# Turning a chunk's keys and scoring them in one TensorE product, with queries and identity side by side

## The chip, the core and the metric

One core of a Trainium2 chip runs the whole program. The metric is device time in microseconds (us) of one execution, the median of several runs. Engines are named as the profile names them: PE is TensorE's matmul, PEld its weight load, DVE is VectorE, ACT is ScalarE, POOL is GpSimd, SP is SyncE, which issues most DMAs.

## The reference

One streaming step of a layer: a SwiGLU half step, a mixer with eight heads (four mLSTM, four retention), an output projection, a second SwiGLU half step and a final norm, for 512 prompt frames and 32 sample frames with a model width of 1024. All in float32. The part that the change touches, for one chunk of one retention head:

```python
scores = einsum('bhtd,bhsd->bhts', q, k) * decay
inner = einsum('bhts,bhse->bhte', scores, v)
out = inner + cross[:, :, None] * einsum('bhtd,bhde->bhte', q, R)
tail = exp(lg[:, None] * (L - 1.0 - idx))
R_new = exp(lg * L)[:, None, None] * R + einsum('hs,bhsd,bhse->bhde', tail, k, v)
```

An mLSTM head has the same shape of work, with weights from its gates in place of `decay` and `tail`, and a normaliser beside the state.

## The kernel before

Activations lie with features on partitions and the T = 544 frames along the free axis; `P` is 128, `NC` is 4 (prompt chunks of 128 frames), `TS` is 32, `H` is 4. Weights arrive by DMA in `w_raw`, ACT rounds them to fp32r (`w_hi`) and DVE makes the remainder (`w_lo`); PE multiplies hi by hi, hi by lo and lo by hi (L763 for whole units of 1024 rows, L887 for the blocks of the feed-forward parts). Each engine's instructions stand in an order written out by hand, with semaphores between engines.

**The mixer** is a loop over eight heads. For each, PE makes four units: queries (u=0), keys (1), values (2), gate (3), each of 48 matmuls of 272 columns. DVE evicts a unit to `proj[:, h % 2, SLOT[what], :]`; in a retention head, queries and keys pass through `rot` and a GpSimd addition as well. The small work of a head is laid between the units of the next: `step_scores(h)` follows its own unit 3, `step_updates(h)` follows unit 0 of the next head, `step_mix(h)` unit 1, `step_turn(h)` the first product of unit 3. For the last head the output projection's units stand between.

**`step_scores` on PE** (L1064 on) fills the four PSUM banks of `X`: bank 0 the four chunks of keys, turned to frames on partitions (transposes against `ident`, L1087); bank 1 the values, turned (L1089); bank 2 the sample frames' keys and values (L1090, L1091) and the sample scores (L1094); bank 3 the chunks' scores, plain f32 products of keys and queries (L1093). The last of them raises `scores_done`.

**What reads them.** DVE's `step_scores` multiplies the scores by weights or decay into `scores` (L2277, L2286), makes the sample's entries (L2278, L2287, L2282, L2288, L2290) and, in mLSTM heads, the key tails `k_tail` (L2281), then raises `scores_weighted`. ACT's `step_values` copies the values to `v_tok` (L1597) and, in retention heads, makes the key tails first (L1595), then raises `v_ready`. The scores and tails are one buffer, `score_tail`, in the profile's names. PE's `step_updates` (L1103) waits for both and writes banks 0 and 1; DVE's `step_states` (L2305 on) follows.

**GpSimd** builds the mixer's constants once behind the first feed-forward part: `mask`, `sel` and a row of memsets, the last of which raises `mixer_consts`; ACT and DVE wait for that. `ident` lies beside `sq_sum` in `sum_ident` and is built at the program's start.

Of the kernel before, what the change touches and what calls it, by code (L numbers as in the profile page):

```python
# [7 lines left out]
ALU = mybir.AluOpType  # L8
ACT = mybir.ActivationFunctionType
# [3 lines left out]
P = 128  # L13
H = 4
# [30 lines left out]
def hybrid_trunk_step(nc, x_prompt, x_sample, state_mlstm_C, state_mlstm_n, state_mlstm_m, state_ret_R,  # L45
# [4 lines left out]
    TP, D = x_prompt.shape[1], x_prompt.shape[2]  # L50
    TS = x_sample.shape[1]
    T = TP + TS
# [4 lines left out]
    NC = TP // P  # L57
    CH = [slice(c * P, (c + 1) * P) for c in range(NC)] + [slice(TP, T)]
# [140 lines left out]
    with ExitStack() as ctx:  # L199

        at = {"next": -(-nc.sbuf_base // 32) * 32}

        def sb(name, shape, dt=F32):
            handle = nc.alloc_sbuf_tensor_at(name, shape, dt, offset=at["next"])
            at["next"] += -(-int(np.prod(shape[1:])) * 4 // 32) * 32
            return handle

        def sem(name):
            return ctx.enter_context(nc.semaphore(name))
# [9 lines left out]
        sq_sum, ident = sum_ident[:, 0:T], sum_ident[:, T:T + P]  # L219
# [82 lines left out]
        sel = sb("sel", [H, H, P])  # L302
        assert at["next"] <= y_ret_end
        at["next"] = y_ret_end
        proj = sb("proj", [P, 2, 4, T])
        table = sb("table", [P, tables.shape[1]])
        sel_r = sb("sel_r", [H, H, P], F32R)
        row_all = sb("row_all", [P, 2, T])
# [6 lines left out]
        weights = sb("weights", [P, T])  # L315
# [6 lines left out]
        scores = score_tail[:, 0:T]  # L322
        k_tail = score_tail[:, T:T + (NC + 1) * P].rearrange("p (c d) -> p c d", d=P)
        v_tok = sb("v_tok", [P, NC + 1, V1])
# [7 lines left out]
        assert at["next"] <= after_y_f  # L332
        at["next"] = after_y_f
        mask = sb("mask", [P, P])
        key_col = sb("key_col", [P, NC + 1, H])
        neg_m_exp = sb("neg_m_exp", [P, NC + 1, H])
        m_prev_all = sb("m_prev_all", [P, H, NC + 1])
        stats = sb("stats", [P, NC + 1, 6])
        mean_var = sb("mean_var", [P, NC + 1, 2])
        small = sb("small", [P, 7, NC + 1])  # L340
        mixer_end = at["next"]
        at["next"] = max(ffn_end, mixer_end)
        assert U_IN % RAW == 1 and 1 not in RAW_READ
# [7 lines left out]
        TAIL, TAIL_S = CROSS + H * P, CROSS + H * P + H  # L351
# [4 lines left out]
        X = ctx.enter_context(nc.psum_tensor("core_banks", [P, 4, 512], F32))  # L356
# [39 lines left out]
        SLOT = (3, 1, 2, 0)  # L396

        def projected(h, what):
            return proj[:, h % 2, SLOT[what], :]

        def sample_block(h, what):
            flat = proj[:, h % 2, :, :].rearrange("p a t -> p (a t)")
            a = SLOT[what] * T + TP
            return flat[:, a:a + P]
# [112 lines left out]
        table_loaded = sem("table_loaded")  # L517
        mixer_consts = sem("mixer_consts")
# [68 lines left out]
        def chained(eng, s):  # L587

            count = [0]

            def link(ins):
                count[0] += 1
                ins.then_inc(s, 1)
                eng.wait_ge(s, count[0])

            return link
# [153 lines left out]
        def _(pe):  # L750
# [317 lines left out]
            def p(h, what, cols):  # L1068
                return projected(h, what)[:, cols]

            def step_scores(h):


                if h >= H:
                    pe.wait_ge(rotated, 2 * (h - H) + 2)
                pe.wait_ge(evicted, T_IN + 4 * h + 3)
                if h:

                    pe.wait_ge(normed, h)
                    pe.wait_ge(normed_act, h)  # L1080
                else:
                    pe.wait_ge(past_ready, 1)
                if h:

                    pe.wait_ge(y_ready, h)
                for c in range(NC):
                    nc.tensor.transpose(X[:, 0, CH[c]], p(h, 1, CH[c]), ident[:, :])  # L1087
                for c in range(NC):
                    nc.tensor.transpose(X[:, 1, CH[c]], p(h, 2, CH[c]), ident[:, :])  # L1089
                nc.tensor.transpose(X[:, 2, 0:P], sample_block(h, 1), ident[:, :])  # L1090
                nc.tensor.transpose(X[:, 2, P:2 * P], sample_block(h, 2), ident[:, :])  # L1091
                for c in range(NC):
                    nc.tensor.matmul(X[:, 3, CH[c]], p(h, 1, CH[c]), p(h, 0, CH[c]), start=True, stop=True)  # L1093
                nc.tensor.matmul(X[:, 2, 2 * P:2 * P + TS], sample_block(h, 1), p(h, 0, CH[NC]),  # L1094
                                 start=True, stop=True).then_inc(scores_done, 1)

# [61 lines left out]
            for h in range(2 * H):  # L1158
                for u in range(4):
                    s, t = U_IN + 4 * h + u, T_IN + 4 * h + u  # L1160
# [56 lines left out]
        def _(act):  # L1217
            link = chained(act, act_step)
# [334 lines left out]
            c, half = X_BY_ACT  # L1553
            a = half * DT // 2
# [30 lines left out]
            def step_values(h):  # L1585
                act.wait_ge(scores_done, h + 1)
                if h:
                    act.wait_ge(mixed_done, h)
                if h == 0:
                    act.wait_ge(mixer_consts, 1)  # L1590
                if h == H:
                    act.wait_ge(table_loaded, 16)
                if h >= H:

                    nc.scalar.activation(k_tail[:, 0:NC, :], X[:, 0, :].rearrange("p (c d) -> p c d", c=NC), ACT.Copy,  # L1595
                                         scale=table[:, TAIL + h - H:TAIL + h - H + 1])
                nc.scalar.activation(v_tok[:, 0:NC, 0:P], X[:, 1, :].rearrange("p (c d) -> p c d", c=NC), ACT.Copy)\  # L1597
                    .then_inc(v_ready, 1)

            def step_gate(h):  # L1600
                act.wait_ge(evicted, T_IN + 4 * h + 4)
                if h:
                    act.wait_ge(y_ready, h)
                nc.scalar.activation(gate_act[:, :], projected(h, 3), ACT.Sigmoid if h < H else ACT.Silu)\
                    .then_inc(gate_act_ready, 1)
# [92 lines left out]
        def _(dve):  # L1698
            link = chained(dve, dve_step)
# [467 lines left out]
            for c, half in X_BY_DVE:  # L2167
                dve.wait_ge(x_moved, X_PIECES.index((c, half)) + 1)
                if c < NC:
                    tiles = dense[c % 2][:, half, :].rearrange("p (k d) -> p k d", d=P)  # L2170
                    a = half * DT // 2
# [98 lines left out]
            def step_scores(h):  # L2270
                dve.wait_ge(scores_done, h + 1)
                if h:
                    dve.wait_ge(mixed_done, h)
                grid = lambda ap: ap.rearrange("p (c d) -> p c d", c=NC)
                if h < H:
                    dve.wait_ge(weights_ready, h + 1)
                    nc.vector.tensor_tensor(scores[:, 0:TP], X[:, 3, :], weights[:, 0:TP], ALU.mult)  # L2277
                    nc.vector.tensor_tensor(scores[0:TS, TP:T], X[0:TS, 2, 2 * P:2 * P + TS], weights[0:TS, TP:T], ALU.mult)  # L2278

                    keep = grid(weights[:, 0:TP])[:, :, P - 1:P].broadcast_to([P, NC, P])  # L2280
                    nc.vector.tensor_tensor(k_tail[:, 0:NC, :], grid(X[:, 0, :]), keep, ALU.mult)  # L2281
                    nc.vector.tensor_scalar(k_tail[0:TS, NC, :], X[0:TS, 2, 0:P], weights[0:TS, T - 1:T], None, ALU.mult)  # L2282
                else:
                    d = DECAY + (h - H) * P
                    decay = table[:, d:d + P].rearrange("p (c d) -> p c d", c=1)
                    nc.vector.tensor_tensor(grid(scores[:, 0:TP]), grid(X[:, 3, :]), decay.broadcast_to([P, NC, P]), ALU.mult)  # L2286
                    nc.vector.tensor_tensor(scores[0:TS, TP:T], X[0:TS, 2, 2 * P:2 * P + TS], table[0:TS, d:d + TS], ALU.mult)  # L2287
                    nc.vector.tensor_scalar(k_tail[0:TS, NC, :], X[0:TS, 2, 0:P],  # L2288
                                            table[0:TS, TAIL_S + h - H:TAIL_S + h - H + 1], None, ALU.mult)
                nc.vector.tensor_copy(v_tok[0:TS, NC, 0:P], X[0:TS, 2, P:2 * P]).then_inc(scores_weighted, 1)  # L2290
# [89 lines left out]
            for h in range(2 * H):  # L2380
                for u in range(4):
                    s, t = U_IN + 4 * h + u, T_IN + 4 * h + u
# [49 lines left out]
        def _(pool):  # L2432
            link = chained(pool, pool_step)

            def triangle(ap, pattern, op, fill, base=0, mult=1):
                return nc.gpsimd.affine_select(out=ap, in_=ap, compare_op=op, fill=fill, base=base, pattern=pattern,
                                               channel_multiplier=mult)
# [56 lines left out]
            pool.wait_ge(w_lo_ready, U_IN + 1)  # L2494
            link(nc.gpsimd.memset(mask[:, :], 0.0))
            link(triangle(mask[:, :], [[1, P]], ALU.is_ge, -1e30, mult=-1))
            link(nc.gpsimd.memset(sel[:, :, :], 1.0))
            link(triangle(sel[:, :, :], [[-1, H], [0, P]], ALU.is_equal, 0.0))
            nc.gpsimd.memset(row_cols[:, :], 0.0)
# [105 lines left out]
```

## Time and profile before

| what | us |
| --- | --- |
| median of 3 runs | 1048.03 (1047.66 to 1048.28) |
| the profiled execution | 1047.74 |
| its span, first to last instruction | 1046.0 |
| PE busy in the span | 1033.6 |
| DVE, ACT, POOL busy | 791.3, 515.1, 215.8 |
| mixer's heads in the span | some 380 to 632 |

The span is what the trace covers; 1.74 us of the execution lie outside of it. Matmuls overlap, so a table's mean of one matmul is longer than its share of the time; the chain of waits lists pieces from start to start.

### The profile page before, as it was taken

Reading aid. Unit: us, or ns where it says so; the run is one execution under the profiler, and the core shown is the slowest. Engines: PE = TensorE matmul, PEld = TensorE weight load, DVE = VectorE, ACT = ScalarE, POOL = GpSimd, SP = SyncE. Lnnn points to the kernel's source line nnn. Section 1 sums busy time; section 2 is a strip of 40 time slices with the busy share of each in tenths; the row PEclk is TensorE's granted clock in tenths of the full one; section 3 lists DMA queues with packets and bytes.
Section 4 is the critical chain, followed back from the end, with each engine's and each line's share of the span. In section 5 each row is a group of like instructions: output and inputs, shape, how many; then the busy total and the mean of one; then the engine's idle time right before and its main releaser. Section 6 shows DMA issues by size and latency. Waiting matters only on the chain.

```text
span 1046.0 us, 20867 instructions
## 1 busy us (share of the span) xinstructions
PE 1033.6 (99%) x8229; PEld 1025.3 (98%) x8229; DVE 791.3 (76%) x1497; ACT 515.1 (49%) x943; POOL 215.8 (21%) x190
## 2 busy tenths in 40 slices
PE   9999999999999999999999999999999999999996
PEld 8999999999999999999999999999999999999996
DVE  5985689997899986555755556588568899789996
ACT  6453366644666664433232223445336664466654
POOL 1100221212122111310332223210012222221210
PEclk9999999999999999999999999999999999999998
DMA  7447787878878466445354223543777888887852
GB/s 226 115 80 181 173 178 167 181 171 174 179 163 172 100 136 137 79 65 84 65 81 76 68 79 62 142 91 86 177 162 165 172 175 170 178 178 167 175 107 97
DMA packets 217051, 142.13 MB, mean 136 GB/s; under 512 B 8685, under 2 KB 214677, under 8 KB 216825
## 3 DMA queue, kind: packets, MB, share of 16 engines
q1 hardware_dynamic: 160824, 110.98, 40.3%
q0 software_dynamic: 56048, 29.79, 22.3%
q8 instruction: 66, 1.08, 0.4%
q14 instruction: 33, 0.26, 0.1%
q10 hardware_dynamic: 80, 0.02, 0.0%
HBM read 135.80 MB, written 3.29 MB: 133 GB/s over the span
## 4 chain that ended last, share of the span: by engine, by line
PE 92%; DVE 3%; issue 2%; DMA 2%; ACT 1%; SPq 0%; DVEq 0%; ACTq 0%
PE dense L887 41%; PE dense L763 35%; PE core_banks L887 6%; PE core_banks L763 3%; PE dense L833 1%; PE core_banks L1118 1%; PE core_banks L1103 1%; DMA sum_ident<-sq 1%; PE core_banks L1121 1%; PE core_banks L1093 1%; DMA x_tok<-in_x_prompt 1%; DVE h_op L1811 1%; DVE w_lo L1769 1%; DVE h_raw L1799 0%; PE core_banks L1130 0%
## 5 line engine op out<-in xcount | busy, mean ns | idle before, releaser
L1306 ACT ACTIVATE w_hi<-w_src 128x512 fp32r<-128x512 f32 x182 | 113.2, 628 | 97.8 <-PE dense L887 55.7
L1306 ACT ACTIVATE w_hi<-w_raw 128x512 fp32r<-128x512 f32 x182 | 112.4, 629 | 77.6 <-PE dense L887 52.1
L887 PE MATMUL dense<-h_op,w_hi 128*128 128x272 f32 x768 | 147.8, 291 | 0.8 <-DVE h_op L1811 0.8
L1769 DVE TENSOR_TENSOR w_lo<-w_src,w_hi 128x512 fp32r<-128x512 f32 x182 | 124.6, 689 | 29.9 <-ACT w_hi L1306 28.1
L1769 DVE TENSOR_TENSOR w_lo<-w_raw,w_hi 128x512 fp32r<-128x512 f32 x182 | 123.9, 688 | 29.0 <-ACT w_hi L1306 27.0
L763 PE MATMUL dense<-xg_hi,w_hi 128*128 128x272 f32 x672 | 141.6, 292 | 0.0
L763 PE MATMUL dense<-xg_hi,w_lo 128*128 128x272 f32 x672 | 138.4, 288 | 0.0
L763 PE MATMUL dense<-xg_lo,w_hi 128*128 128x272 f32 x672 | 138.1, 287 | 0.0
L887 PE MATMUL dense<-x_late_hi,w_hi 128*128 128x272 f32 x432 | 125.7, 291 | 0.0
L887 PE MATMUL dense<-x_op_hi,w_lo 128*128 128x272 f32 x432 | 124.6, 288 | 0.0
L887 PE MATMUL dense<-x_late_hi,w_lo 128*128 128x272 f32 x432 | 124.5, 288 | 0.0
L887 PE MATMUL dense<-x_op_hi,w_hi 128*128 128x272 f32 x432 | 124.4, 288 | 0.0
L887 PE MATMUL dense<-x_late_lo,w_hi 128*128 128x272 f32 x432 | 124.1, 287 | 0.0
L887 PE MATMUL dense<-x_op_lo,w_hi 128*128 128x272 f32 x432 | 124.1, 287 | 0.0
L887 PEld LDWEIGHTS dense<-h_op,w_hi 128*128 128x128 f32 x768 | 120.1, 188 | 3.3 <-DVE xT L1898 2.8
L1713 DVE TENSOR_TENSOR w_lo<-w_raw,w_hi 128x1024 fp32r<-128x1024 f32 (+1 forms) x69 | 86.3, 1251 | 38.1 <-ACT w_hi L1252 37.9
L887 PE MATMUL dense<-h_op,w_lo 128*128 128x272 f32 x384 | 110.7, 288 | 0.0
L763 PEld LDWEIGHTS dense<-xg_lo,w_hi 128*128 128x128 f32 x672 | 105.1, 188 | 0.0
L763 PEld LDWEIGHTS dense<-xg_hi,w_lo 128*128 128x128 f32 x672 | 104.8, 189 | 0.0
L763 PEld LDWEIGHTS dense<-xg_hi,w_hi 128*128 128x128 f32 x672 | 104.6, 189 | 0.1
L1252 ACT ACTIVATE w_hi<-w_raw 128x1024 fp32r<-128x1024 f32 (+1 forms) x69 | 68.9, 1000 | 30.8 <-PE dense L763 17.2
L887 PEld LDWEIGHTS dense<-x_late_hi,w_hi 128*128 128x128 f32 x432 | 81.2, 188 | 2.1 <-DVE rstd L1844 2.1
(363 smaller groups left out, 2389.4 us busy)
## 6 DMA issues: line engine op xcount, KB each, us to landing
w_raw<-in_w_ffn_up SPq DMA_DIRECT2D x43, 512.0 KB, 5.0
w_src<-in_w_ffn_gate SPq DMA_DIRECT2D x36, 512.0 KB, 5.2
w_raw<-in_w_in SPq DMA_DIRECT2D x31, 512.0 KB, 8.4
w_src<-in_w_ffn_gate POOLq DMA_DIRECT2D x36, 256.0 KB, 5.5
w_raw<-in_w_ffn_up POOLq DMA_DIRECT2D x36, 256.0 KB, 6.0
w_src<-in_w_ffn_down SPq DMA_DIRECT2D x16, 512.0 KB, 5.3
w_raw<-in_w_ffn_down SPq DMA_DIRECT2D x16, 512.0 KB, 5.2
w_raw<-in_w_ffn_down SPq DMA_DIRECT2D x16, 384.0 KB, 5.8
```

What stands on the lines that cost most here:

```text
L763: last = nc.tensor.matmul(out[:, half, 0:TH], w[:, s % 4, k, :], x(kt)[:, half * TH:(half + 1) * TH], start=start and n == 0 and m == 0, s ...
L833: last = nc.tensor.matmul(bank_of(u)[:, half, 0:TH], w[:, u, k, :], x(k)[:, half * TH:(half + 1) * TH], start=part == "hh" and k == 0, sto ...
L887: last = nc.tensor.matmul(out, w[:, k, :], x, start=o in OPENS and k == 0 and m == 0, stop=k == KH - 1 and m == 2, skip_group_check=o not ...
L1093: nc.tensor.matmul(X[:, 3, CH[c]], p(h, 1, CH[c]), p(h, 0, CH[c]), start=True, stop=True)
L1103: last = nc.tensor.matmul(X[:, b, o * V1:(o + 1) * V1], k_tail[:, c, :], v_tok[:, c, :], start=True, stop=True)
L1118: last = nc.tensor.matmul(out, score_tail[:, block], v_tok[:, c, :], start=True, stop=c == 0)
L1121: last = nc.tensor.matmul(out, sum_ident[:, block], state, start=False, stop=True)
L1252: nc.scalar.activation(w_hi[:, s % 4, 0:k_tiles(s), :], raw, ACT.Copy).then_inc(w_hi_ready, 1)
L1306: nc.scalar.activation(block_of(w_hi, n, o), source(e, o), ACT.Copy).then_inc(block_hi, 1)
L1713: nc.vector.tensor_tensor(w_lo[:, s % 4, 0:nk, :], unit_raw(s), w_hi[:, s % 4, 0:nk, :].bitcast(F32), ALU.subtract).then_inc(w_lo_ready, 1)
L1769: nc.vector.tensor_tensor(block_of(w_lo, n, o), source(g % 2, o), block_of(w_hi, n, o).bitcast(F32), ALU.subtract)\
L1811: nc.vector.tensor_tensor(lo, h_source(k, o), hi.bitcast(F32), ALU.subtract).then_inc(h_op_lo_ready, 1)
```

## The change

The identity gets a second copy, `ident_near`, right behind `proj` in one buffer, `proj_wide`, built by GpSimd. A chunk's key product then has keys as the stationary operand and a moving operand of two pieces of 128 columns, queries and identity, so that one plain product of 256 columns writes the chunk's scores and its turned keys side by side. `KEY_CHUNKS` spans banks 0 and 1 of `X`; the values move to bank 3. PE's four key transposes and four score products per head become four such products. PE waits for `mixer_consts` before the first head's. In retention heads the key tails move from ACT to DVE. The small per-chunk tables are packed into one buffer (`minis`), which makes room for the second identity.

```diff
-        proj = sb("proj", [P, 2, 4, T])
+        proj_region = at["next"]
+        proj_wide = sb("proj_wide", [P, 2 * (2 * 4 * T + P) - 3 * T])
+        proj = proj_wide[:, 0:2 * 4 * T].rearrange("p (n a t) -> p n a t", n=2, a=4)
+        ident_near = proj_wide[:, 2 * 4 * T:2 * 4 * T + P]
+        at["next"] = proj_region + (2 * 4 * T + P) * 4
...
+        minis = sb("minis", [P, (NC + 1) * (3 * H + 15)])
...
+        def query_and_ident(h, c):
+
+            q = (h % 2) * 4 * T + SLOT[0] * T + c * P
+            stride = 2 * 4 * T - q
+            return proj_wide[:, q:q + 2 * stride].rearrange("p (a s) -> p a s", a=2)[:, :, 0:P]
+
+        KEY_CHUNKS = X[:, 0:2, :].rearrange("p a b -> p (a b)").rearrange("p (c a d) -> p c a d", c=NC, a=2)
+        SCORES_OF, KEYS_OF = KEY_CHUNKS[:, :, 0, :], KEY_CHUNKS[:, :, 1, :]
...
+                if h == 0:
+                    pe.wait_ge(mixer_consts, 1)
                 for c in range(NC):
-                    nc.tensor.transpose(X[:, 0, CH[c]], p(h, 1, CH[c]), ident[:, :])
+                    nc.tensor.matmul(KEY_CHUNKS[:, c, :, :], p(h, 1, CH[c]), query_and_ident(h, c), start=True, stop=True)
                 for c in range(NC):
-                    nc.tensor.transpose(X[:, 1, CH[c]], p(h, 2, CH[c]), ident[:, :])
+                    nc.tensor.transpose(X[:, 3, CH[c]], p(h, 2, CH[c]), ident[:, :])
                 nc.tensor.transpose(X[:, 2, 0:P], sample_block(h, 1), ident[:, :])
                 nc.tensor.transpose(X[:, 2, P:2 * P], sample_block(h, 2), ident[:, :])
-                for c in range(NC):
-                    nc.tensor.matmul(X[:, 3, CH[c]], p(h, 1, CH[c]), p(h, 0, CH[c]), start=True, stop=True)
...
-                if h == H:
-                    act.wait_ge(table_loaded, 16)
-                if h >= H:
-
-                    nc.scalar.activation(k_tail[:, 0:NC, :], X[:, 0, :].rearrange("p (c d) -> p c d", c=NC), ACT.Copy,
-                                         scale=table[:, TAIL + h - H:TAIL + h - H + 1])
-                nc.scalar.activation(v_tok[:, 0:NC, 0:P], X[:, 1, :].rearrange("p (c d) -> p c d", c=NC), ACT.Copy)\
+                nc.scalar.activation(v_tok[:, 0:NC, 0:P], X[:, 3, :].rearrange("p (c d) -> p c d", c=NC), ACT.Copy)\
...
-                    nc.vector.tensor_tensor(scores[:, 0:TP], X[:, 3, :], weights[:, 0:TP], ALU.mult)
+                    nc.vector.tensor_tensor(grid(scores[:, 0:TP]), SCORES_OF, grid(weights[:, 0:TP]), ALU.mult)
...
-                    nc.vector.tensor_tensor(k_tail[:, 0:NC, :], grid(X[:, 0, :]), keep, ALU.mult)
+                    nc.vector.tensor_tensor(k_tail[:, 0:NC, :], KEYS_OF, keep, ALU.mult)
...
-                    nc.vector.tensor_tensor(grid(scores[:, 0:TP]), grid(X[:, 3, :]), decay.broadcast_to([P, NC, P]), ALU.mult)
+                    nc.vector.tensor_tensor(grid(scores[:, 0:TP]), SCORES_OF, decay.broadcast_to([P, NC, P]), ALU.mult)
...
+                    nc.vector.tensor_scalar(k_tail[:, 0:NC, :], KEYS_OF, table[:, TAIL + h - H:TAIL + h - H + 1], None, ALU.mult)
...
+            link(nc.gpsimd.memset(ident_near[:, :], 0.0))
+            link(triangle(ident_near[:, :], [[-1, P]], ALU.not_equal, 1.0))
```

## Rows read from the trace of the kernel before

**Rows 1.** The page: busy time by engine; shares of the chain that ended last.

```profile
PE 1033.6 (99%) x8229; PEld 1025.3 (98%) x8229; DVE 791.3 (76%) x1497; ACT 515.1 (49%) x943; POOL 215.8 (21%) x190
...
PE 92%; DVE 3%; issue 2%; DMA 2%; ACT 1%; SPq 0%; DVEq 0%; ACTq 0%
```

**Rows 2.** PE's waits over the whole span: us in total, times, longest.

```profile
PE dense L1057 <- DMA x_tok<-in_x_prompt: 1.3, 1, 1.3
PE dense L1024 <- ACT x_gain L1496: 1.2, 1, 1.2
PE core_banks L1024 <- DVE xT L1898: 1.2, 1, 1.2
...
PE dense L763 <- issue: 0.3, 1, 0.3
```

**Rows 3.** Busy time by stretch (us, instructions in brackets), granted clock, DMA share, GB/s.

```profile
core 0: us, PE busy (x) PEld busy (x) DVE busy (x) ACT busy (x) POOL busy (x), PEclk, DMA share, GB/s
...
526.00:556.00 30.00, 30.00 (x248) 30.00 (x248) 17.59 (x39) 8.36 (x11) 10.14 (x7) 1.00 0.50 82
...
sum 240.00, PE 240.00 PEld 239.72 DVE 137.94 ACT 75.35 POOL 56.93; mean PE 26.67 PEld 26.64 DVE 15.33 ACT 8.37 POOL 6.33
```

**Rows 4.** Chain of waits, a retention head's scores and updates: start, us, what.

```profile
526.25 0.44 PE core_banks L1087 x4
...
527.34 0.89 PE core_banks L1093 x8
528.23 0.14 PE core_banks L1094 x2
...
534.45 1.11 PE core_banks L1103 x10
```

**Rows 5.** PE by line and shape: xcount | busy us, mean ns of one | idle before.

```profile
L1093 PE MATMUL core_banks<-proj 128*128 128x128 f32 x64 | 8.5, 275 | 0.0
...
L1087 PE MATMUL core_banks<-sum_ident,proj 128*128 128x128 f32 x32 | 4.8, 272 | 0.0
```

**Rows 6.** Chain of waits at the second feed-forward block's norm sums.

```profile
674.20 0.92 PE core_banks L808 x4
```

**Rows 7.** Instructions in time, same head: DVE, then ACT; start, us, what [idle before].

```profile
528.41 0.69 DVE L2286 TENSOR_TENSOR score_tail<-core_banks,table 128x512 f32<-128x512 f32 x1 [1.27 <-PE core_banks L1094]
...
529.38 0.27 DVE L2290 COPY v_tok<-core_banks 32x128 f32<-32x128 f32 x1
530.57 1.23 DVE L1713 TENSOR_TENSOR w_lo<-w_raw,w_hi 128x1024 fp32r<-128x1024 f32 x1 [0.92 <-ACT w_hi L1252]
...
528.41 0.69 ACT L1595 ACTIVATE score_tail<-core_banks,table 128x512 f32<-128x512 f32 x1 [3.48 <-PE core_banks L1094]
529.00 0.59 ACT L1597 ACTIVATE v_tok<-core_banks 128x512 f32<-128x512 f32 x1
```

**Rows 8.** Instructions in time, DVE, in an mLSTM head.

```profile
498.62 0.71 DVE L2210 TENSOR_TENSOR proj<-dense,rstd 128x544 f32<-128x544 f32 x1
...
499.95 0.67 DVE L2281 TENSOR_TENSOR score_tail<-core_banks,weights 128x512 f32<-128x512 f32 x1
```

**Rows 9.** Last head: chain of waits at the updates; DVE in time.

```profile
620.96 1.11 PE core_banks L1103 x10
...
618.87 0.27 DVE L2290 COPY v_tok<-core_banks 32x128 f32<-32x128 f32 x1
```

**Rows 10.** Instructions in time, mixer's start: GpSimd, then ACT's first user.

```profile
379.89 0.20 POOL L2495 MEMSET mask<- 128x128 f32 x1 [11.33 <-DVE w_lo L1713]
...
381.12 0.52 POOL L2497 MEMSET sel<- 4x512 f32 x1
...
383.57 0.10 POOL L2509 MEMSET state_in<- 128x4 f32 x1
...
393.16 0.61 ACT L1659 ACTIVATE sel_r<-sel 4x512 fp32r<-4x512 f32 x1
```

More of the change, by code:

```diff
@@ L334, in hybrid_trunk_step @@
         mask = sb("mask", [P, P])
[L335 to L340, printed above, removed]
+        tables_of = {}
+        minis = sb("minis", [P, (NC + 1) * (3 * H + 15)])
+        first = 0
+        for name, inner in (("key_col", H), ("neg_m_exp", H), ("stats", 6), ("mean_var", 2)):
+            tables_of[name] = minis[:, first:first + (NC + 1) * inner].rearrange("p (c a) -> p c a", a=inner)
+            first += (NC + 1) * inner
+        for name, outer in (("m_prev_all", H), ("small", 7)):
+            tables_of[name] = minis[:, first:first + (NC + 1) * outer].rearrange("p (a c) -> p a c", a=outer)
+            first += (NC + 1) * outer
+        key_col, neg_m_exp, m_prev_all = (tables_of[name] for name in ("key_col", "neg_m_exp", "m_prev_all"))
+        stats, mean_var, small = (tables_of[name] for name in ("stats", "mean_var", "small"))
         mixer_end = at["next"]
```

## The prediction, made before the changed kernel ran

> **What bounds the kernel now.** Read the page's busy shares and its chain of work first [rows 1]: TensorE (PE) is busy for 1033.6 of 1046.0 us and carries 92% of the chain that ended last. A busy PE is not by itself a bound, so read PE's waits over the whole span next [rows 2]: there are six lines of them, 5.9 us in all (the first three and the last are shown), and the three longest are PE's first work (L1057, input frames) and its last (L1024, the turned output). None belongs to a line of the mixer's heads. The table by stretches confirms it [rows 3]: over the nine stretches from 400 to 640 us PE is busy for 240.00 of 240 us, and in the one shown, as in the others, the granted clock is 1.00 (the higher level, 2.4 GHz), while VectorE (DVE) is busy for about 58% and ScalarE (ACT) for about 31% (137.94 and 75.35 of 240.00). So in the mixer, time is PE's time: an operation that PE gains moves the end by its spacing to the next, and an operation that DVE or ACT gains or loses costs nothing until PE waits for it.
>
> The durations of single matmuls (0.27 us) overlap, so they are of no use as prices. The chain of waits gives start-to-start pieces, and its pieces for one head [rows 4] are the prices: four key turns (L1087) 0.44 us, the four score products (L1093) 0.89. The score products have eight instructions: the table by line [rows 5] has 64 for 32 products (L1093), but 32 for 32 turns (L1087). A plain f32 product is thus two passes over its columns, each with its own weight load, and a turn is one. That gives 0.44/4 = 0.110 us for a turn and 0.89/8 = 0.111 us for a pass of 128 columns.
>
> **The change on PE.** Per head it removes the four key turns and the four score products, 0.44 + 0.89 = 1.33 us; the value turns stay, into another bank. It adds four plain f32 products of 256 columns, eight passes. What is a pass of 256 f32 columns worth? The trace has one wide f32 product: the norm's sums at L808, two halves of 272 columns, four passes in 0.92 us [rows 6], 0.230 each. Between 0.111 at 128 columns and 0.230 at 272 the line has a slope of 0.119/144 = 0.00083 us a column, so 256 columns take 0.111 + 128 x 0.00083 = 0.217 us; 0.230 x 256/272 gives the same. Eight of them: 1.736 us. The head therefore pays 1.736 - 1.33 = +0.41 us. The saved weight loads bring nothing, since they ran under the columns: the pass of 32 columns at L1094 takes 0.14/2 = 0.07 us [rows 4], so a load with its product fits into 0.07, and 0.111 at 128 columns is the columns' own time. In short, keys are no longer turned in the one-pass mode but in the two-pass mode of a product, and that doubles the turn: 4 x (0.217 - 0.110) = 0.43, less a few nanoseconds of spacing per instruction. Eight heads: 8 x 0.406 = **+3.2 us**.
>
> No row shows a moving operand in two pieces as far apart as queries and identity. At the dear end it runs as two pieces of 128: 0.222 a pass, 64 x 0.222 - 8 x 1.33 = +3.6 us. A gain would need a pass under 1.33/8 = 0.166, and 272 columns took 0.230, so that end is left to rival 1. I take +3.2, by L808, the nearest row in width and type.
>
> Beside the row stands a rule: the Trainium skill ("TensorE: Matmul & The Clock Gate", Terms) calls the transpose mode four times faster for FP32. It speaks against this change as the rows do, but its factor is not theirs: rows 4 make it 0.222/0.110 = 2 for 128 columns; with its factor the same edit would cost 32 x (0.440 - 0.110) = +10.6 us (an estimate from that page).
>
> **DVE and ACT.** In the four retention heads ACT loses the key tail (L1595, 0.69 us) and DVE gains it. The nearest DVE rows are the same step's products from PSUM with as many elements: 0.69 (L2286) [rows 7] and 0.67 (L2281) [rows 8]. I take +0.7; the low end is the 0.27 of L2290, which has a quarter of the columns. Cover: before, DVE's last step (L2290) ends at 529.38 + 0.27 = 529.65 and ACT's copy of the values at 529.00 + 0.59 = 529.59, and PE wants both only at 534.45, when the updates (L1103) start [rows 4, 7]. With +0.7 DVE ends at 530.35, 4.1 us early. The next instruction in DVE's queue, a w_lo (L1713), starts at 530.57 after 0.92 us of waiting for ACT's w_hi, which stands behind the work that ACT loses; so it isn't later either. The tightest case is the last head, where only half a unit of products stands between: updates at 620.96, DVE's end at 618.87 + 0.27 = 619.14 [rows 9]. With +0.7 for DVE, and PE's extra 0.41 shifting both sides alike, 1.1 us remain. Price: 0. If the cover were gone, 4 x 0.7 = 2.8 us. In the four mLSTM heads DVE's operations stay; they read other places in PSUM, in rows of 128 with gaps, as the eviction L2210 already reads two pieces in two banks: 0.71 us for 544 [rows 8], no dearer per element than L2281. Price: 0.
>
> **GpSimd and the new wait.** Two more instructions build the second identity behind the mask. Mask's pair takes from 379.89 to 381.12, when sel's starts: 1.23 us [rows 10]. The last memset, which raises mixer_consts, goes from 383.57 to 384.80. The first user of mixer_consts is ACT's sel_r at 393.16: 8 us of cover. DVE waits for it ahead of the gate rows; behind the memset in GpSimd's queue stands a DMA of these very rows, and PE, whose wait is new, stands before the first head's scores, behind products that need them (L1138, L1146). So the condition is met when PE comes to it, though all of PE's later work stands behind that wait. Price: 0, or 1.2 us once without cover. No DMA is added or moved; the 512 bytes by which later buffers shift, and the small tables packed into one, change no instruction.
>
> **Sum.** Profiled execution: 1047.74 us with a span of 1046.0, so 1.74 lie around it. New span 1046.0 + 3.2 = 1049.2, execution 1050.9. The median of the runs is 0.29 above that execution: **1051.2 us**.
>
> **Rivals.**
> 1. Weight loads set the pass. If 0.111 us were the load and not the columns, a pass of 256 would cost no more than one of 128: eight passes 0.89, and the change would save the four turns, 8 x 0.44 = 3.5 us: 1044.5, faster. It decides wherever a load is longer than the columns' time. For it: the load rows are as busy as the product rows [rows 3]. Against it: 0.07 at 32 columns, 0.111 at 128 and 0.230 at 272 grow with columns. Chance 0.04. The Trainium skill's same page (Back-to-back issue gap) has sustained pairs grow from about 81 to 131 ns between 128 and 512 columns, which leans to this side; rows 4 and 6 do not agree with it for f32, where twice the columns take twice the time.
> 2. The added time is taken up elsewhere. If PE's 0.41 a head replaced a wait further on, the end would move by 1 us or less: 1048 to 1049, no measurable change. For it: some waits exist. Against it: none is in the mixer, and the few behind it hang on PE's own results, which come later by the same amount [rows 2]. Chance 0.05.
> 3. DVE becomes late. If the key tails had no cover, the updates of four heads would wait 0.7 each: 1051.2 + 2.8 = 1054.0. Against it: 1.1 to 4.1 us of slack. Chance 0.03.
> 4. Turning by plain product costs four times a turn rather than twice (the rule above as a mechanism: 0.440 for a 128-column product). 1058.6. Against it: score products of the same type cost 0.222. Chance 0.01.
>
> **How the numbers follow.** Forecast, +2.6 to +4.0 us: 0.87. A change of 0.2% (2.1 us) is about what a measurement of this kernel can tell from none. Slower: forecast 0.87 + rival 3 0.03 + rival 4 0.01 = 0.91. Same: rival 2, 0.05, and 0.01 of rival 1, for loads that set a part of the pass: 0.06. Faster: the rest of rival 1, 0.03. Range: 3.2 less 0.7 (a slightly cheaper pass, and the 0.3 us by which the runs lie about their median) to 3.6 plus 0.5: 1050.3 to 1052.2. The rivals outside it hold 0.13.
>
> **What the profile after would show.** The new product line: 64 PE instructions of 128x256, eight in about 1.74 us of the chain; 128x128 would mean that it was split. The 32-column pair stays at 0.14; a head grows by 0.4 us. PE should still have no wait in the mixer; a wait at the updates for DVE's score_tail or v_tok would be rival 3. GpSimd's last memset should end near 384.9. If eight wide passes take clearly under 1.33 us, or if PE idles before them in the first head, the prediction is wrong in its main step.

## The result, and the profile after

The changed kernel took 1050.48 us (median of 15 runs, 1050.09 to 1052.74) against 1048.03 for the kernel before (median of 15), a ratio of 1.0024 with a 95% interval of 1.0018 to 1.0031: some 2.5 us slower, between 1.9 and 3.2. Forecast were 1051.2 us and a range of 1050.3 to 1052.2. The profiled execution took 1050.64 us with a span of 1048.9, so 2.9 more than the one before.

The page first: busy time by engine, and the shares of the chain (compare [rows 1]).

```profile
PE 1037.3 (99%) x8197; PEld 1027.1 (98%) x8197; DVE 794.0 (76%) x1501; ACT 512.5 (49%) x939; POOL 215.0 (21%) x192
...
PE 93%; DVE 3%; issue 2%; DMA 1%; ACT 0%; SPq 0%; DVEq 0%
```

PE has 32 instructions fewer and is busy 3.7 us longer; DVE has four more and ACT four fewer. PE's waits over the whole span (us in total, times, longest; compare [rows 2]):

```profile
PE dense L1042 <- ACT x_gain L1514: 1.2, 1, 1.2
PE core_banks L1059 <- POOL ones L2452: 1.1, 1, 1.1
PE dense L781 <- issue: 1.0, 1, 1.0
PE core_banks L1042 <- DVE xT L1910: 0.8, 1, 0.8
PE dense L905 <- DVE h_op L1823: 0.8, 4, 0.2
PE dense L1075 <- DMA x_tok<-in_x_prompt: 0.3, 1, 0.3
```

No wait lies in the mixer, and the new one for mixer_consts isn't among them. (L781 makes the heads' units too, but its one wait here is at 81.88 us, in the first feed-forward part; the 0.3 of L763 in [rows 2] is at 82.63.) Three lines are not as before. The first frames' load (0.3 for 1.3) and this wait of L781 (1.0 for 0.3) differ between profiles of one kernel as well: before_again, below, has 0.6 and 0.5. The third is the wait for xT at the end, 0.8 (L1042), which was 1.2 (L1024), though the change doesn't touch it. More on that below.

The same retention head as in [rows 4], in the chain of waits (start, us, what); under it the wide product's line in the table by line and shape (compare [rows 5]):

```profile
527.77 1.73 PE core_banks L1107 x8
529.50 0.44 PE core_banks L1109 x4
...
530.16 0.14 PE core_banks L1112 x2
530.30 6.06 PE dense L781 x48
536.36 1.11 PE core_banks L1121 x10
...
L1107 PE MATMUL core_banks<-proj_wide 128*128 128x256 f32 x64 | 15.1, 379 | 0.0
```

Eight passes of 256 columns take 1.73 us, 0.216 each; before, key turns and score products took 0.44 + 0.89 = 1.33. So a head pays 0.40. The norm's sums bracket the mixer, and the chain gives where each begins, in the kernel before and then in the changed one (the second row of before is in [rows 6]):

```profile
378.69 1.18 PE core_banks L808 x4
```

```profile
378.62 1.19 PE core_banks L826 x4
...
677.33 0.92 PE core_banks L826 x4
```

Before 674.20 - 378.69 = 295.51 us, after 677.33 - 378.62 = 298.71: **+3.20 us**, against a forecast of 8 x 0.406 = 3.2.

The same head on DVE and then on ACT, in order of time (compare [rows 7]), and the last head's end on DVE with the chain's updates (compare [rows 9]):

```profile
530.34 0.69 DVE L2298 TENSOR_TENSOR score_tail<-core_banks,table 128x512 f32<-128x512 f32 x1 [1.69 <-PE core_banks L1112]
...
531.04 0.73 DVE L2300 TENSOR_SCALAR score_tail<-core_banks,table 128x512 f32<-128x512 f32 x1
...
531.96 0.27 DVE L2303 COPY v_tok<-core_banks 32x128 f32<-32x128 f32 x1
532.16 1.20 DVE L1725 TENSOR_TENSOR w_lo<-w_raw,w_hi 128x1024 fp32r<-128x1024 f32 x1
...
530.34 0.60 ACT L1609 ACTIVATE v_tok<-core_banks 128x512 f32<-128x512 f32 x1 [3.90 <-PE core_banks L1112]
...
622.68 0.27 DVE L2303 COPY v_tok<-core_banks 32x128 f32<-32x128 f32 x1
...
624.09 1.11 PE core_banks L1121 x10
```

The key tail takes DVE 0.73 us (0.66 to the next start); DVE is done at 532.23, 4.1 us ahead of the updates at 536.36, and in the last head at 622.95, 1.1 us ahead of 624.09. GpSimd in order of time (compare [rows 10]):

```profile
381.05 0.21 POOL L2510 MEMSET proj_wide<- 128x128 f32 x1
381.40 0.29 POOL L2449 TENSOR_SCALAR_AFFINE_SELECT proj_wide<-proj_wide 128x128 f32<-128x128 f32 x1
...
384.21 0.10 POOL L2524 MEMSET state_in<- 128x4 f32 x1
```

The second identity takes 0.70 us, to the next start at 381.75, and not 1.23 as the mask's pair; the last memset, at 384.21, is still far ahead of ACT's first use of the constants (at 393.1 in this profile too) and of PE's first wide product (406.7). The nearer row for it was the select that builds the first identity at the program's start: 0.29 us at 1.55 us in the kernel before, against 0.81 for the mask's.

### The profile page after: what moved, and what is told of

Its sections match the earlier page's. It is cut to its first block, busy times and chain, and to the rows that moved or that the text cites. A ratio compares the mean times of both kernels' runs of the same rounds, so it can differ in the third digit from the quotient of the medians.

```text
span 1048.9 us, 20806 instructions
## 1 busy us (share of the span) xinstructions
PE 1037.3 (99%) x8197; PEld 1027.1 (98%) x8197; DVE 794.0 (76%) x1501; ACT 512.5 (49%) x939; POOL 215.0 (21%) x192
## 4 chain that ended last, share of the span: by engine, by line
PE 93%; DVE 3%; issue 2%; DMA 1%; ACT 0%; SPq 0%; DVEq 0%
PE dense L905 42%; PE dense L781 35%; PE core_banks L905 6%; PE core_banks L781 3%; PE core_banks L1107 1%; PE dense L851 1%; PE core_banks L1136 1%; PE core_banks L1121 1%; PE core_banks L1139 1%; DMA x_tok<-in_x_prompt 1%; DVE h_op L1823 1%; DVE w_lo L1781 1%; DVE h_raw L1811 0%; PE core_banks L1148 0%; PE core_banks L1109 0%
## 5 line engine op out<-in xcount | busy, mean ns | idle before, releaser
L781 PE MATMUL dense<-xg_hi,w_hi 128*128 128x272 f32 x672 | 141.4, 292 | 0.0
L781 PE MATMUL dense<-xg_hi,w_lo 128*128 128x272 f32 x672 | 138.5, 288 | 0.0
L781 PE MATMUL dense<-xg_lo,w_hi 128*128 128x272 f32 x672 | 138.1, 287 | 0.0
L781 PEld LDWEIGHTS dense<-xg_lo,w_hi 128*128 128x128 f32 x672 | 105.1, 188 | 0.0
L781 PEld LDWEIGHTS dense<-xg_hi,w_lo 128*128 128x128 f32 x672 | 104.8, 189 | 0.0
L781 PEld LDWEIGHTS dense<-xg_hi,w_hi 128*128 128x128 f32 x672 | 104.6, 188 | 0.1
```

What stands on the lines that cost most here:

```text
L781: last = nc.tensor.matmul(out[:, half, 0:TH], w[:, s % 4, k, :], x(kt)[:, half * TH:(half + 1) * TH], start=start and n == 0 and m == 0, s ...
```

## The experiments

**Theory**: the whole cost is PE's columns, since a key is now turned in two passes and not in one; everything else hides. **Rivals**: weight loads set the pass; the two pieces of the moving operand cost something; DVE is late; the rest of the change gives something back (the median rose by 2.45, not by 3.2).

Two stretches are read for each kernel, from its profile's chain of waits: from the first norm sums to the second (the mixer and the output projection), and from there to the span's end. They are collected here; the rows behind the first lines stand above.

| kernel | first norm sums at | between the sums | to the end |
| --- | --- | --- | --- |
| before | 378.69 | 295.51 | 371.80 |
| before_again, before_third | 379.32, 378.43 | 295.51, 295.51 | 371.77, 371.76 |
| changed | 378.62 | 298.71 | 371.57 |
| after_again | 378.27 | 298.71 | 371.42 |
| turns_back | 378.26 | 295.52 | 371.52 |
| narrow | 378.32 | 299.13 | 371.55 |
| half_pieces | 382.18 | 292.81 | 371.51 |
| tails_only, tails_only_timed | 378.78, 378.82 | 295.49, 295.48 | 371.53, 371.50 |
| layout_only | 379.10 | 295.49 | 371.81 |
| tails_thrice, tails_four, tails_five | 381.40, 377.69, 378.63 | 299.44, 300.23, 302.57 | 371.66, 371.48, 371.50 |

### PE's part undone: turns_back

```diff
-                    nc.tensor.matmul(KEY_CHUNKS[:, c, :, :], p(h, 1, CH[c]), query_and_ident(h, c), start=True, stop=True)
+                    nc.tensor.transpose(KEYS_OF[:, c, :], p(h, 1, CH[c]), ident[:, :])
...
+                for c in range(NC):
+                    nc.tensor.matmul(SCORES_OF[:, c, :], p(h, 1, CH[c]), p(h, 0, CH[c]), start=True, stop=True)
```

> Everything of the change stays (layout, banks, second identity, DVE's key tails, the new wait) but PE's instructions: key turns in transpose mode and score products apart, written to the new places. Theory (the whole cost is PE's columns): 0.44 + 0.89 us a head again, 1048.0 us, within 0.4 of the kernel before. Rival (the rest of the change gives something back, which would explain why the median rose by 2.45 and not by 3.2): 1047.3, 0.7 below the kernel before. Rival (the rest costs, by DVE or the new wait): above 1048.5.

Measured: 1048.32 us (median of 11), ratio to the kernel before 0.9998 (0.9986 to 1.0010). One of the eleven executions took 2014.33 us, and nothing on record says why. In the chain of waits the head's pieces are the old ones; behind them stand the two norm sums:

```profile
525.82 0.44 PE core_banks L1107 x4
...
526.91 0.89 PE core_banks L1113 x8
...
378.26 1.19 PE core_banks L826 x4
...
673.78 0.92 PE core_banks L826 x4
```

Between the sums it has 295.52 us, as before. So PE's edit carries the whole cost, and banks, DVE's tails and the new wait carry none in the mixer. By time it can't be told from the kernel before; the 0.3 us that its profile gains lie behind the mixer.

### Width alone: narrow

```diff
-                    nc.tensor.matmul(KEY_CHUNKS[:, c, :, :], p(h, 1, CH[c]), query_and_ident(h, c), start=True, stop=True)
+                    nc.tensor.matmul(SCORES_OF[:, c, :], p(h, 1, CH[c]), p(h, 0, CH[c]), start=True, stop=True)
+                    nc.tensor.matmul(KEYS_OF[:, c, :], p(h, 1, CH[c]), ident_near, start=True, stop=True)
```

> The changed kernel with each wide product split in two of 128 columns, keys by queries and keys by identity, so 16 passes a head with 16 weight loads in place of 8. Theory (columns set the time, loads hide): 16 x 0.111 = 1.78 us a head against 1.73, so 0.4 us above the changed kernel, 1050.9. Rival (a load costs of its own, so that the wide product saves some): each of 8 more loads a head costs up to the 0.07 us of the narrowest pass, 8 x 8 x 0.07 = 4.5 us more, 1055. Rival (the two pieces far apart cost the wide product): below the changed kernel.

Measured: 1051.50 us (median of 12), ratio to the kernel before 1.0036 (1.0022 to 1.0050). In the chain each product is two passes again, 0.22 for two of 128 columns; then the norm sums:

```profile
527.69 0.22 PE core_banks L1107 x2
527.92 0.22 PE core_banks L1108 x2
...
378.32 1.18 PE core_banks L826 x4
...
677.45 0.92 PE core_banks L826 x4
```

299.13 us between the sums: 0.42 above the changed kernel for 64 more passes with their loads, 0.007 us each. What these 0.007 us are isn't shown; a weight load that cost time of its own, up to 4.5 us in all by the rival, is excluded. Putting queries and identity side by side thus saves 0.4 us over doing the same with two products; it is the identity product itself that costs.

### Two pieces: half_pieces

```diff
+                    w = P // 2 if h else P
-                    nc.tensor.matmul(KEY_CHUNKS[:, c, :, :], p(h, 1, CH[c]), query_and_ident(h, c), start=True, stop=True)
+                    nc.tensor.matmul(KEY_CHUNKS[:, c, :, 0:w], p(h, 1, CH[c]), query_and_ident(h, c)[:, :, 0:w], start=True, stop=True)
```

> The changed kernel with only the first 64 queries and the first 64 identity columns as pieces in heads 1 to 7, so 128 columns in two pieces; half of each chunk's scores and turned keys is left out there. Theory (columns alone): a pass takes 0.111 us as with one piece of 128, 0.89 us in place of 1.73 in seven heads, 5.9 us below the changed kernel, 1044.6. Rival (the step between the pieces costs): eight passes take more than 0.89. Rival (PE does not set the end in the mixer): less than half of the 5.9 us shows in the end.

Measured: 1044.63 us (median of 11), ratio to the kernel before 0.9960 (0.9945 to 0.9975). The piece of the chain in the same head, and the norm sums:

```profile
528.81 0.89 PE core_banks L1108 x8
...
382.18 1.18 PE core_banks L826 x4
...
674.99 0.92 PE core_banks L826 x4
```

0.89 us for eight passes of twice 64 columns, the same as for eight of 128 in one piece [rows 4], so the step between the pieces costs nothing that these rows could show. Between the sums 292.81 us, 5.9 under the changed kernel, and all of it reaches the end. With 0.07, 0.111, 0.216 and 0.230 us for 32, 128, 256 and 272 columns, rival 1 of the prediction is excluded: from 128 columns on, the columns set a pass. At 32 they do not, since the slope from 128 to 272 columns would give some 0.03 (an estimate from 0.111 and 0.230).

### How much DVE's cover bears: tails_five, tails_four, tails_thrice

```diff
+                    for _ in range(4):
+                        link(nc.vector.tensor_scalar(k_tail[:, 0:NC, :], KEYS_OF, table[:, TAIL + h - H:TAIL + h - H + 1], None, ALU.mult))
                     nc.vector.tensor_scalar(k_tail[:, 0:NC, :], KEYS_OF, table[:, TAIL + h - H:TAIL + h - H + 1], None, ALU.mult)
```

(3 and 2 in place of 4 for the other two.)

> The changed kernel with DVE making the key tails of a retention head's chunks five times instead of once, 4 x 0.72 = 2.9 us more on DVE in each of four heads. Theory (a cover of 4.1 us in three heads and 1.1 us in the last): the first three hide it, the updates of the last head come 1.8 us later, so 1.8 us above the changed kernel, 1052.3. Rival (DVE's later work, the next weights' low parts, has no cover): 4 x 2.9 = 11.6 us more, 1062. Rival (DVE has room everywhere): 1050.5.

Measured: 1054.44 us (median of 5, 1053.46 to 1055.79), 4.0 above the changed kernel where 1.8 were expected: a miss. The place was right: PE waits once, before the last head's updates, and three heads hide 3 us more of DVE. From PE's waits, then PE in order of time at that place, then the busy time by stretch (PE, PEld, DVE, ACT, POOL, granted clock, DMA share, GB/s):

```profile
PE core_banks L1121 <- DVE v_tok L2305: 2.0, 1, 2.0
...
626.15 2.52 PE L1121 MATMUL core_banks<-v_tok,score_tail 128*128 128x129 f32 x10 [2.04 <-DVE v_tok L2305]
...
610.00:624.00 14.00, 14.00 (x109) 13.62 (x107) 8.68 (x13) 5.40 (x8) 3.82 (x3) 1.00 0.26 77
624.00:627.00 3.00, 0.96 (x5) 0.86 (x5) 2.02 (x5) 0.00 (x0) 0.00 (x0) 0.85 0.00 0
627.00:630.00 3.00, 3.00 (x17) 3.00 (x17) 1.20 (x5) 0.00 (x0) 0.00 (x0) 0.58 0.00 0
630.00:634.00 4.00, 4.00 (x36) 4.00 (x36) 1.91 (x6) 0.00 (x0) 0.00 (x0) 1.00 0.38 112
```

PE was at full clock up to the wait. Behind it the granted clock is 0.58 from 627 to 630, and asked in finer stretches it is 1.00 from 624 to 626, while PE waits, and 0.50, its lower level of 1.2 GHz, from 626.15 to 629. The updates take 2.52 us there. So the wait cost twice: its own length, and what the lower clock took. The next two runs set the length of the wait lower.

> The changed kernel with the key tails of retention heads made four times by DVE: 3 x 0.77 = 2.3 us more, so a wait of 1.2 us before the last head's updates. Theory (a wait of this length leaves the clock at its higher level): 1.2 us above the changed kernel. Rival (the clock falls behind it as behind the wait of 2.0 us): 1.2 + 1.8 = 3.0 us above.

> The changed kernel with the key tails of retention heads made three times by DVE: 2 x 0.77 = 1.5 us more, against a cover of 1.1 us in the last head. With five times, PE waited 2.0 us there and then ran at the lower clock, so that the end came 3.9 us later. Theory (a wait costs its length, the fall of the clock comes only with a longer one): a wait of 0.4 us, 0.4 above the changed kernel, clock 1.00 behind it. Rival (any wait there costs the clock): 0.4 + 1.8 = 2.2 us above.

Measured: 1052.52 us for four (median of 5, 1051.13 to 1055.04) and 1051.41 for three (median of 5, 1050.89 to 1054.19), beside 1050.76 for the changed kernel on the same chip: 1.8 and 0.7 above. PE at the same place, four and then three:

```profile
624.42 1.38 PE L1121 MATMUL core_banks<-v_tok,score_tail 128*128 128x129 f32 x10 [1.25 <-DVE v_tok L2305]
```

```profile
627.35 1.38 PE L1121 MATMUL core_banks<-v_tok,score_tail 128*128 128x129 f32 x10 [0.47 <-DVE v_tok L2305]
```

The updates take 1.38 us behind either wait, so the clock holds (1.00 in the stretches behind it, in these two profiles). From the last head's scores to the product of 276 matmuls that follows the output projection's start, the chain has 24.24 us in the changed kernel, 24.98 for three, 25.76 for four and 28.12 for five. That is 0.74 for a wait of 0.47, 1.52 for 1.25 and 3.88 for 2.04: in the first two the wait and 0.27, by which the updates behind it are longer (1.38 against 1.11), and in the third some 1.57 more, of which the updates have 2.52 - 1.38 = 1.14 and the 18 matmuls behind them 2.68 - 2.26 = 0.42. Each of the two theories held in part: the short waits cost 0.27 us more than their length, the long one nearly twice its length. The runs of four reach 1055.04, and whether the clock fell in those isn't known, since only one run has a profile. The profiled execution of three took 1054.19, but not by this place: its first norm sums begin late, at 381.40 (see Scatter).

### What the rest gives back: after_again, before_again, before_third, tails_only, layout_only

No edit in the first three: the changed kernel and the kernel before, profiled again.

> The changed kernel once more, unaltered, against the kernel before on one chip. Theory (the mixer costs 3.2 us and the rest is scatter at the start and the end of an execution): the stretch between the two norm sums is again 298.7 us against 295.5, and the median lies 2.5 to 3.5 above the kernel before. Rival (something outside the mixer gives 0.7 back): the median is again some 2.4 above, and the stretches outside the mixer are shorter than before by as much.

Measured: 1050.76 us (median of 6) against 1047.86, ratio 1.0030 (1.0019 to 1.0042); between the sums 298.71 us once more. The 3.20 us of the mixer are the same to 0.01 in both profiles. Both medians, +2.45 and +2.90, lie below that.

> The kernel before, unaltered, profiled again. In its first profile the stretch from the second norm sums to the end took 371.8 us, in every profile of the new layout 371.4 to 371.7. Theory (scatter from one execution to the next): a second profile shows some 371.5 too, and the change costs 3.2 us wherever it is read. Rival (the new layout shortens the end by 0.3): 371.8 again, and the change costs 2.9.

> The kernel before once more, as a third profile of the same question: 371.5 us from the second norm sums to the end by scatter, 371.8 by layout; the stretch between the two norm sums is 295.5 us by both.

Measured: 371.77 and 371.76 us to the end. So the kernel before is 0.3 us longer behind the mixer in each of three profiles, and the rival holds: 0.3 are given back. Here is the place, VectorE (DVE) in order of time at the end, in the third profile of before and then in the changed kernel:

```profile
1032.46 0.42 DVE L2065 TENSOR_TENSOR sq_last<-sq_last 128x256 f32<-128x256 f32 x1
1033.35 0.43 DVE L2065 TENSOR_TENSOR sq_last<-sq_last,sum_ident 128x256 f32<-128x256 f32 x1 [0.46 <-DVE sq_last L2065]
```

```profile
1035.95 0.43 DVE L2077 TENSOR_TENSOR sq_last<-sq_last 128x256 f32<-128x256 f32 x1
1036.48 0.43 DVE L2077 TENSOR_TENSOR sq_last<-sq_last,sum_ident 128x256 f32<-128x256 f32 x1
```

Between the two sums of squares stood 0.89 us before and stand 0.53 now. The profile puts the second's wait of 0.46 us down to the first sum, but that had ended when the wait began; in the changed kernel the second starts 0.10 us behind the first's end. DVE's next work, an update of xT, then comes 0.36 later in the kernel before, and that is PE's wait for xT of 1.2 us, now 0.8. To see what part of the change does it, its other parts were put into the kernel before one at a time:

```diff
-                if h >= H:
-
-                    nc.scalar.activation(k_tail[:, 0:NC, :], X[:, 0, :].rearrange("p (c d) -> p c d", c=NC), ACT.Copy,
-                                         scale=table[:, TAIL + h - H:TAIL + h - H + 1])
...
+                    nc.vector.tensor_scalar(k_tail[:, 0:NC, :], grid(X[:, 0, :]), table[:, TAIL + h - H:TAIL + h - H + 1], None, ALU.mult)
```

> The kernel before with one part of the change alone: the retention heads' key tails made by DVE (four more DVE instructions, four fewer on ACT); banks, layout and PE as before. All three profiles of the kernel before have a DVE gap of 0.46 us ahead of the second sum of squares at the end (L2065), and 371.8 us from the second norm sums to the end; profiles of the changed layout have neither. Theory (it hangs on DVE's instruction stream, which is four longer): gap gone, 371.5 us, between the norm sums 295.5. Rival (it hangs on the layout): gap still there, 371.8.

and, in the other kernel, `proj_wide`, `minis` and the two GpSimd instructions, as in the change:

```diff
+        proj_wide = sb("proj_wide", [P, 2 * (2 * 4 * T + P) - 3 * T])
...
+        minis = sb("minis", [P, (NC + 1) * (3 * H + 15)])
...
+            link(nc.gpsimd.memset(ident_near[:, :], 0.0))
+            link(triangle(ident_near[:, :], [[-1, P]], ALU.not_equal, 1.0))
```

> The kernel before with the other parts alone: buffer layout, packed small tables and GpSimd's second identity, which nothing reads; PE, DVE and ACT as before. Theory (DVE's instruction stream): the gap of 0.46 us and 371.8 us stay. Rival (layout): gap gone, 371.5 us. By both 295.5 us between the norm sums, and GpSimd's two instructions cost nothing.

The same DVE instruction in tails_only, then in layout_only:

```profile
1033.36 0.43 DVE L2059 TENSOR_TENSOR sq_last<-sq_last,sum_ident 128x256 f32<-128x256 f32 x1
```

```profile
1033.99 0.42 DVE L2074 TENSOR_TENSOR sq_last<-sq_last,sum_ident 128x256 f32<-128x256 f32 x1 [0.46 <-DVE sq_last L2074]
```

With the tails on DVE the gap is gone and the end takes 371.53 us; with the layout alone it stays, 371.81. So moving the four tails gives the 0.3 back: DVE's stream has four instructions more ahead of this place, and ACT's four fewer. Which of the two does it no run separates; since DVE is the engine that stands, its own stream is the nearer candidate. Why DVE stands for 0.4 us at one instruction isn't shown: the profile names no releaser that fits. Both expectations named the outcome; between the sums both have 295.49 us, so neither part costs anything there, GpSimd's two instructions included.

> The kernel before with only the key tails of the retention heads moved to DVE, now timed. The gap of 0.46 us at the end is gone in its profile and PE's work is that of the kernel before, so theory: 0.3 us below the kernel before, ratio 0.9997, less than a comparison of this kernel can tell from nothing. Rival (the tails on DVE cost in other executions, where the heads come closer): above 1.000.

Measured: 1047.45 us (median of 11) against 1047.66, ratio 0.9994 (0.9985 to 1.0003). By time it can't be told from the kernel before.

**Scatter.** The first norm sums began anywhere from 377.69 us (tails_four) to 382.18 (half_pieces). In the profiles of half_pieces and of tails_thrice PE waits in the first feed-forward part, where nothing was changed. Here is that wait, and the busy time of the stretch with it, in half_pieces and then in tails_thrice:

```profile
PE dense L905 <- DVE x_late_lo L1802: 2.0, 1, 2.0
...
60.00:80.00 20.00, 17.87 (x141) 17.44 (x140) 15.63 (x23) 11.65 (x20) 0.00 (x0) 1.00 0.34 39
```

```profile
PE dense L905 <- DVE x_late_lo L1801: 2.1, 1, 2.1
...
60.00:80.00 20.00, 17.93 (x131) 17.62 (x130) 14.90 (x21) 11.44 (x20) 0.00 (x0) 0.91 0.34 40
```

In both the chain leads from there back to a weight load (w_raw from w_ffn_up) that took 15.5 us to land; the list of transfers of the changed kernel has medians of 3.2 to 6.1 for loads of this tensor. These executions took 1048.24 and 1054.19 us where the medians of their kernels are 1044.63 and 1051.41. The rows also bear on the clock: behind a wait of 1.99 us (half_pieces) it held at 1.00, behind one of 2.07 (tails_thrice) it was 0.50 from 72 to 75 us, as behind the 2.04 of tails_five. Three waits of so nearly one length, with two outcomes, don't show what decides. For a question of 3 us, a stretch of the trace between two fixed places, the same to 0.04 us in profiles that run the same PE work (295.48 to 295.52 in seven), answered what medians left between 1.9 and 4.4.

## Why the prediction was right

**The bound.** It holds: PE works through the mixer without a wait, and what it gains there the end gains. Turns_back and half_pieces took 3.2 and 5.9 us of the changed kernel's PE work away, and the second norm sums came as much earlier behind the first.

**The price of the wide pass.** Interpolated 0.217 us between 128 and 272 columns, measured 0.216; per head 0.41, measured 0.40; eight heads 3.2, measured 3.20. The step that mattered was to price a pass from start to start, and to see that a turn is one pass and a plain product two. The dear end for the two pieces (3.6) was not needed: pieces cost nothing. Narrow, at +3.62 between the sums, shows what it would have been.

**The rule weighed.** The Trainium skill ("TensorE: Matmul & The Clock Gate", Terms) has the transpose mode four times faster for FP32. The runs agree on the direction and not on the factor: for 128 columns, 0.22 us for two passes of a product (narrow) against 0.11 for a turn (turns_back).

**The rivals.** Weight loads (0.04) are excluded by narrow and half_pieces. The added time taken up elsewhere (0.05) failed as put: nothing behind the mixer replaces a wait. A late DVE (0.03) did not come true; its slack was forecast as 4.1 and 1.1 us and is 4.1 and 1.1, and tails_five shows that the last head is where it ends. Four times a turn (0.01) is excluded by the 1.73 us.

**What was off.** The median lies 0.7 under the forecast: +2.45 over the kernel before, below the +2.6 to +4.0 that the prediction gave its 0.87, while the second comparison's +2.90 lies inside. That 1050.48 is inside the stated range is partly luck: the range's own terms, 3.2 less 0.7 over the median of 1048.03, give a low end of 1050.5 and not 1050.3. The mechanism is confirmed by the 3.20 us of the traces, not by that. Of the 0.7 that the forecast was too high, about 0.3 are in the step that priced the DVE edit at 0 because nothing in the mixer waited for it: the move of the four tails took away a gap of 0.4 us at the very end, in no view of the mixer, but to be read in the kernel before as a DVE gap that no releaser explains. The other 0.4 are scatter as far as the runs can tell: 3.20 - 0.3 = 2.9 is the difference of the profiled executions and of the second comparison's medians, and lies in the interval of the first. The second identity was sized at 1.23 us by the mask's pair and took 0.70; it hid either way. "None belongs to a line of the mixer's heads" holds for the place and not for the line, since L763, with its 0.3, makes the heads' units too. DVE's key tail was sized at 0.7 and took 0.73.

## What to carry to other kernels

Where PE is the bound, count passes and columns, not instructions: a product by the identity turns a tile at the price of a plain f32 product, twice that of a transpose here, and sharing the weight load saved only 0.007 us a pass. Price an instruction by its start-to-start piece in the chain at two widths; here that held, to 0.001 us, for a third between them. For effects of some us in a kernel of a thousand, compare a stretch between two fixed places of the traces before comparing medians.

## What the runs showed of the hardware that was not expected

- A wait of 0.47 or 1.25 us of a PE that ran at 2.4 GHz until then cost its length and 0.27 us; a wait of 2.04 us cost 3.9, as the granted clock fell to 0.50 behind it. Behind one of 2.07 in another run it fell to 0.50 too, and behind one of 1.99 it stayed at 1.00.
- A DVE instruction at the end stood 0.46 us idle in all three profiles of the kernel before and in layout_only, and in none of the kernels with the key tails moved to DVE; the cause is open.
- A moving operand in two pieces, far apart in memory, streams as fast as one piece: 0.89 us for eight passes of 128 columns either way.
